# One block for RWKV-7's tables and its scan, whole triangles of T, and one keys product a pair, in a hybrid encoder step

## The reference

```python
def step(S, inp):
    r_t, w_t, k_t, v_t, a_t, b_t = inp
    sa = jnp.einsum('bhij,bhj->bhi', S, a_t)
    S = S * w_t[:, :, None, :] + sa[..., None] * b_t[:, :, None, :] + v_t[..., None] * k_t[:, :, None, :]
    return S, jnp.einsum('bhij,bhj->bhi', S, r_t)
```

## Time and profile before

| what | us |
|---|---|
| median of 3 runs | 3667.14 |
| profiled execution | 3673.35 |
| its span | 3671.6 |
| TensorE, busy | 3480.9 (95%) |
| VectorE, ScalarE, GpSimd, busy | 1516.0, 1133.6, 603.4 |

### The profile page before, as it was taken

One profiled execution on the slowest core, in us unless ns is written; L12 is line 12 of the kernel. 1 busy time (PEld: TensorE's weight loads), 2 busy tenths in 40 slices (PEclk: granted clock), 3 DMA queues, 4 the chain that ended last, 5 costly groups with the idle time before them and its releaser, 6 DMA issues. The chain is left out here.

```text
span 3671.6 us, 60425 instructions
## 1 busy us (share of the span) xinstructions
PE 3480.9 (95%) x25874; PEld 3264.4 (89%) x25874; DVE 1516.0 (41%) x2519; ACT 1133.6 (31%) x2132; POOL 603.4 (16%) x724
## 2 busy tenths in 40 slices
PE   8899979999999999998899996987999999999998
PEld 8898769989999999995598795866998999999997
DVE  6335464343332332335326666555334332232233
ACT  6323263223220220224535532554223321121123
POOL 1100112002110110111312366423101110010012
PEclk9999989999999999998899997999999999999999
DMA  6411311201111111114646777963200111111111
GB/s 224 114 58 60 106 36 49 81 18 41 47 47 47 47 47 46 47 41 117 226 151 204 244 203 162 246 152 83 92 24 29 47 47 47 46 47 47 47 40 66
DMA packets 461158, 323.17 MB, mean 88 GB/s; under 512 B 108871, under 2 KB 438951, under 8 KB 457607
## 3 DMA queue, kind: packets, MB, share of 16 engines
q1 hardware_dynamic: 405645, 280.65, 26.5%
q10 hardware_dynamic: 44878, 19.14, 2.1%
q0 software_dynamic: 10368, 19.51, 1.6%
HBM read 232.32 MB, written 87.01 MB: 87 GB/s over the span
## 5 line engine op out<-in xcount | busy, mean ns | idle before, releaser
L83 PE MATMUL ps<-am_y,am_wh 128*128 128x352 f32 x4944 | 1182.9, 322 | 16.0 <-PEq L2631 16.0
L83 PE MATMUL ps<-am_h,am_wh 128*128 128x352 f32 x3648 | 887.7, 325 | 1.2 <-DVE am_h L1415 1.2
L83 PEld LDWEIGHTS ps<-am_y,am_wh 128*128 128x128 f32 x4944 | 856.4, 188 | 18.1 <-issue 16.8
L83 PE MATMUL ps<-am_y,am_wl 128*128 128x352 f32 x2472 | 792.8, 321 | 0.0
L83 PEld LDWEIGHTS ps<-am_h,am_wh 128*128 128x128 f32 x3648 | 639.8, 189 | 4.3 <-DVE am_h L1415 1.4
L83 PE MATMUL ps<-am_h,am_wl 128*128 128x352 f32 x1824 | 590.4, 324 | 0.0
L83 PEld LDWEIGHTS ps<-am_y,am_wl 128*128 128x128 f32 x2472 | 464.2, 188 | 0.0
L83 PEld LDWEIGHTS ps<-am_h,am_wl 128*128 128x128 f32 x1824 | 344.3, 189 | 0.0
L1503 POOL TENSOR_TENSOR am_silu<-am_silu,rs 128x352 f32<-128x352 f32 x132 | 126.8, 962 | 1229.2 <-ACT am_silu L1359 1229.2
L1085 DVE TENSOR_TENSOR x<-ps,x 128x352 f32<-128x352 f32 x240 | 125.9, 525 | 466.3 <-PE ps L83 460.7
L917 ACT ACTIVATE am_wh<-am_w 128x1024 fp32r<-128x1024 f32 (+1 forms) x184 | 189.5, 1030 | 378.2 <-PE ps L83 372.9
(11 more groups left out here) (340 smaller groups left out, 4581.3 us busy)
## 6 DMA issues: line engine op xcount, KB each, us to landing
am_w<-in_ffn_w SPq DMA_DIRECT2D x120, 512.0 KB, 3.8
rw_ra_d<-tb_rk SPq DMA_DIRECT2D x8, 1056.0 KB, 7.9
rw_kbt_d<-tb_gk SPq DMA_DIRECT2D x8, 1056.0 KB, 4.3
rw_gg_d<-tb_gk SPq DMA_DIRECT2D x8, 1056.0 KB, 6.5
fr_w<-in_xa_wk SPq DMA_DIRECT2D x8, 1024.0 KB, 5.8
fr_w<-in_xa_wv SPq DMA_DIRECT2D x8, 1024.0 KB, 5.4
am_w<-in_xa_wq SPq DMA_DIRECT2D x16, 512.0 KB, 3.8
am_w<-in_xa_wo SPq DMA_DIRECT2D x16, 512.0 KB, 3.8
```

What stands on the lines that cost most here:

```text
L83: mm = nc.tensor.matmul(out, l, part, start=start and n == 0, stop=stop and n == 2)
```

## The change

Tables and scan become one block: `delta_scan` returns its engine programs and some helpers, and `tables` calls them at the end of its own. Scan tiles lie on the other side of SBUF or in tiles of tables; V, A and g/kbt of tables lie in y. T is kept and stored as whole triangles (chunk, s, t), all six stores of the second batch go by ScalarE's queue, and GpSimd waits for them before it loads T. Rows, keys and the first state are loaded ahead, in a new order. `kbt` in the scan gets 128 columns a pair, zero off the two heads' blocks, cleared by GpSimd, filled by DMAs for each head and chunk (256 B pieces); a pair then takes one 128 by 128 product. Behind the scan, bonus and gate have semaphores of their own. One cleanup moves to the end of the layer.

```diff
-def delta_scan(nc, ps, a, ra_d, g_d, kbt_d, vt_d, tt_d, dec, y, p_out, s_out, x, x_d, ln, ident):
+def delta_scan(nc, ctx, spare, stage, ps, a, ra_d, g_d, kbt_d, vt_d, tt_d, dec, y, p_out, s_out, x, x_d, ln, ident):
...
-        g_in, ra_in, kbt, v = (sb(s, SLOTS, PAIRS, 2, HD) for s in ("g_in", "ra_in", "kbt", "v"))
+    sb = lambda s, *shape, side="right": ctx.enter_context(nc.sbuf_tensor(f"ds_{s}", [P, *shape], F32, side=side))
+    state = stage[:, 0:16 * HD].rearrange("r (n p i) -> r n p i", n=2, i=HD)
...
+    g_in, ra_in, v = (sb(s, SLOTS, PAIRS, 2, HD) for s in ("g_in", "ra_in", "v"))
+    kbt = sb("kbt", SLOTS, PAIRS, 2, 2, HD)
+    ra = sb("ra", 2, PAIRS, 2, 2, C)
+    g = spare[:, 0:32 * HD].rearrange("r (s p a h t) -> r s p a h t", s=2, p=PAIRS, a=2, h=2)
+    tt_cleared, v_cleared, keys_cleared = ([sem(f"{t}_cleared{s}") for s in range(SLOTS)] for t in ("tt", "v", "keys"))
...
+    rest_due = lambda l: 16 * (6 * loads(l) - (2 if l % SLOTS == 0 else 0))
...
+    def clear(ops, at):
+        ops.memset(kbt[:, at], 0.0).then_inc(keys_cleared[at], 1)
+        ops.memset(tt[:, at], 0.0).then_inc(tt_cleared[at], 1)
+        ops.memset(v[:, at], 0.0).then_inc(v_cleared[at], 1)
+
+    def first_clears():
+        for l in range(2):
+            clear(nc.gpsimd, l)
+
+    def load_rows(sp, l):
+        c, w = chunks(l)
+        for t, d in ((g_in, g_d), (ra_in, ra_d)):
+            sp.dma_start(t[:, l % SLOTS, :, 0:w, :], d[:, :, c:c + w, :].rearrange("p r c x -> r p c x"))\
+                .then_inc(rows_in[l % SLOTS], 16)
+
+    def load_keys(sp, l):
+        c, w = chunks(l)
+        if l < SLOTS:
+            sp.wait_ge(keys_cleared[l], 1)
+        for h in range(2):
+            r = slice(h * HD, (h + 1) * HD)
+            for sub in range(w):
+                sp.dma_start(kbt[r, l % SLOTS, :, sub, h, :], kbt_d[:, r, c + sub, :].rearrange("p r x -> r p x"))\
                     .then_inc(rest_in[l % SLOTS], 16)
-                if l < SLOTS:
-                    sp.wait_ge(v_cleared[l], 1)
+
+    def load_state(pool):
+        pool.dma_start(of_head[:], a["c_heads"][1]).then_inc(heads_in, 16)
+        pool.dma_start(by_pair(turned[:, 0]), a["state_rwkv"][0, 0].rearrange("h i j -> i h j")).then_inc(init_in, 16)
...
+    def sync(sp):
+        for l in range(LOADS):
+            c, w = chunks(l)
+            if l >= SLOTS:
+                sp.wait_ge(y_done, last(l - SLOTS) + 1)
+            if l >= SLOTS:
+                load_rows(sp, l)
+                sp.wait_ge(y_done, last(l - SLOTS) + 2)
+                load_keys(sp, l)
+            elif l == 1:
+                load_rows(sp, 2)
+                load_keys(sp, 2)
+            if l < SLOTS:
+                sp.wait_ge(v_cleared[l], 1)
+            for h in range(2):
+                sp.dma_start(v[h * HD:h * HD + C, l % SLOTS, :, 0:w, :],
+                             vt_d[:, h * C:(h + 1) * C, c:c + w, :].rearrange("p s c x -> s p c x"))\
...
+    def gpsimd(pool):
+        for l in range(LOADS):
+            if l >= SLOTS:
+                pool.wait_ge(y_done, last(l - SLOTS) + 1)
+            elif l == 2:
+                clear(nc.gpsimd, l)
+            if l < SLOTS:
+                pool.wait_ge(tt_cleared[l], 1)
+            c, w = chunks(l)
+            s, got = l % SLOTS, tt_in[l % SLOTS]
+            for odd in range(2):
                 for h in range(2):
...
-                    for p in range(4 * q, 4 * q + 4):
-                        for h in range(2):
-                            r, at = side[h], p % 4 * HD
-                            mm = nc.tensor.matmul(ps[r, 2 + 2 * q, at:at + HD], kbt[r, l % SLOTS, p, sub, :], vu[r, p, :],
-                                                  start=True, stop=True)
-                    mm.then_inc(s_done, 1)
+                for p in range(4 * q, 4 * q + 4):
+                    at = p % 4 * HD
+                    mm = nc.tensor.matmul(ps[:, 2 + 2 * q, at:at + HD], kbt[:, l % SLOTS, p, sub].rearrange("r h j -> r (h j)"),
+                                          vu[:, p, :], start=True, stop=True)
+                mm.then_inc(s_done, 1)
+            y_part(n, lambda p: vu[:, p, :], lambda p: g[:, s, p, 1], False).then_inc(y_done, 1)
...
@@ tables @@
-        V, A = sb("v", 2, TOK), sb("a", 2, TOK)
+        V, A = y[:, 0:2], y[:, 2:4]
...
-        rk, gk = sb("rk", 2, NCH, HD), sb("gk", 2, NCH, HD)
+        rk = sb("rk", 2, NCH, HD)
+        gk = y[:, 4:8].rearrange("p k t -> p (k t)").rearrange("p (a c x) -> p a c x", a=2, x=HD)
...
-        rows_x = [t.rearrange("l (s x) -> l s x", s=C) for t in eyes]
-        inv_x = [t.rearrange("l s (a t) -> l a s t", a=per[q]) for q, t in enumerate(rows_x)]
+        inv_x = [t.rearrange("l (a s t) -> l a s t", a=per[q], s=C) for q, t in enumerate(eyes)]
...
             sp.wait_ge(bonus_done, p + 1)
             sp.dma_start(pair_rows(bonus_d, p), extra).then_inc(bonus_out, 16)
+            if p == PAIRS - 1:
+                for b in range(BLOCKS):
+                    groups.wait_summed(sp, 3 * KT - 1, b)
+                sp.wait_ge(ra_stored, 16 * PAIRS)
+                sp.wait_ge(g_stored, 16 * PAIRS)
+                sp.wait_ge(kbt_stored, 16 * PAIRS)
+                load_rows(sp, 0)
             sp.wait_ge(vt_out, 4 * (p + 1))
...
-                nc.gpsimd.memset(eyes[q][:, n * C:n * C + (C - 1) * (per[q] * C + 1) + 1:per[q] * C + 1], 1.0).then_inc(eyes_set[q], 1)
+                nc.gpsimd.memset(eyes[q][:, n * C * C:(n + 1) * C * C:C + 1], 1.0).then_inc(eyes_set[q], 1)
...
-                    eng.dma_start(tt_d[p % 2, h, :, p // 2, g0 * per[q]:g1 * per[q]]
-                                  .rearrange("s (g a) t -> g s (a t)", a=per[q]),
-                                  rows_x[q][x_ * rows + g0:x_ * rows + g1]).then_inc(inv_out, 16)
+                    eng.dma_start(tt_d[p % 2, h, p // 2, g0 * per[q]:g1 * per[q]]
+                                  .rearrange("(g a) s t -> g (a s t)", a=per[q]),
+                                  eyes[q][x_ * rows + g0:x_ * rows + g1]).then_inc(inv_out, 16)
...
             store_v(sp, PAIRS - 1)
-            store_triangles(sp, 1, range(3))
+            load_keys(sp, 0)
+            load_rows(sp, 1)
+            load_keys(sp, 1)
+            sp.wait_ge(vt_stored, 64 * PAIRS)
             sp.wait_ge(bonus_out, 16 * PAIRS)
-            sp.wait_ge(inv_out, 16 * 22)
-            sp.wait_ge(vt_stored, 64 * PAIRS)
-            for t in (ra_stored, g_stored, kbt_stored):
-                sp.wait_ge(t, 16 * PAIRS)
             for b in range(BLOCKS):
                 sp.wait_ge(stored[b], beta_due(PAIRS, b))
+            scan_sync(sp)
 
         @block.tensor
         def _(pe):
...
             turn(PAIRS - 1)
+            pe.wait_ge(g_out, len(PIECES) * PAIRS)
+            pe.wait_ge(kbt_out, len(PIECES) * PAIRS)
+            pe.wait_ge(vt_out, 4 * PAIRS)
+            scan_tensor(pe)
...
-            store_triangles(act, 1, range(3, 6))
+            store_triangles(act, 1, range(6))
+            scan_scalar(act)
...
             steps(52, 2 * (C - 1) - top)
+            dve.wait_ge(added[1], steps_done(1, 1, C - 1))
+            dve.wait_ge(ends, PAIRS)
+            for b in range(BLOCKS):
+                groups.wait_summed(dve, 3 * KT - 1, b)
+            scan_vector(dve)
...
                 substitute(pool, nc.gpsimd, 1, n // (C - 1), n % (C - 1))
+            for b in range(BLOCKS):
+                groups.wait_summed(pool, 3 * KT - 1, b)
+            load_state(pool)
+            first_clears()
+            pool.wait_ge(inv_out, 16 * 22)
+            scan_gpsimd(pool)
...
@@ delta_post @@
             for p in range(n):
-                if p >= 2:
-                    sp.wait_ge(gated, 2 * (p - 1))
-                for j, src in enumerate((bonus_d, g_d)):
+                for j, (src, got, free) in enumerate(((bonus_d, bonus_in, shifted), (g_d, gate_in, gated))):
+                    if p >= 2:
+                        sp.wait_ge(free, 2 * (p - 1))
                     for s in range(2):
                         head = p // 2 * 4 + 2 * s + p % 2
                         sp.dma_start(inp[s * HD:(s + 1) * HD, p % 2, j], src[head * HD:(head + 1) * HD, 0:SEQ])\
-                            .then_inc(tile_in[p % 2], 16)
+                            .then_inc(got[p % 2], 16)
                 if p < 2:
...
-                pool.wait_ge(tile_in[p % 2], 64 * (p // 2 + 1))
+                pool.wait_ge(gate_in[p % 2], 32 * (p // 2 + 1))
...
-                dve.wait_ge(tile_in[p % 2], 64 * (p // 2 + 1))
+                dve.wait_ge(bonus_in[p % 2], 32 * (p // 2 + 1))
...
@@ odd_layer @@
-    lt_d, tt_d = (dram("lt0", 2, 5, NCH, C, C), dram("lt1", 2, 3, PADDED, C, C)), dram("tt", 2, 2, C, PAIRS // 2, PADDED, C)
-    with ExitStack() as mix:
+    lt_d, tt_d = (dram("lt0", 2, 5, NCH, C, C), dram("lt1", 2, 3, PADDED, C, C)), dram("tt", 2, 2, PAIRS // 2, PADDED, C, C)
+    with nc.cleanup_on_exit(), ExitStack() as mix:
...
```

(43 more changed lines are left out.)

319 lines of the change are left out of this document (126 added, 193 removed).

## The result

The change makes the kernel **slower**: 3684.13 us (median of 7 runs, 3678.58 to 3689.56) against 3668.15 (7 runs of the kernel before beside it, 3666.09 to 3673.43), a ratio of 1.0041 with a 95% interval of 1.0031 to 1.0050. The forecast was 3655 with a range of 3646 to 3664.

A forecast was written before the change was run, and what follows sets the result against it. Bounds: the tables-to-scan hand-over, a 4.49 us scan-step chain with TensorE stops, then DVE's load waits. -6 + 1.5 - 0.7 + 0 - 7 + 0.4 = -11.8: profiled 3661.5, median about 3655 us; own range 3651 to 3659, with rivals 3646 to 3664.

The forecast's parts named there:

- the fourth, the keys product: Scan step: 8 products of 128 by 128 take 1.11 us, not 1.15; -0.7 us over 33, ends 0 and -1.5.
- Slower: Scan's key loads: a 256 B packet costs twice a 512 B one, DMA queues become the bound; +15, 3682 us; chance 0.08.
- Keys' loads and fetches: Scan: fewer instruction fetches against 256 B key packets, queue share 0.76 to 0.87; 0 us, ends -2 and +4.
- First batch of T: End of tables, ScalarE's queue: ten whole-triangle stores issue at 0.5 us each, 5 us in all; v chain gains 5.
- One block: Hand-over from tables to scan: chunk 1 starts at 2279.5 instead of 2285.4; -6 us, ends -8 and -3.
- the wait of some 6 us for v 1: Scan's start: TensorE ends chunk 0 at 2273.5, then waits for the v load of chunk 1, landed at 2279.5.
- Clock: Scan's first chunks: TensorE's clock may fall again under chunks 1 and 2; +1.5 us, one such stretch about 3.
- Split semaphores: Stage behind the scan: of DVE's 9.9 us of waits for loads, 3 stay; -7 us, ends -4 and -9.
- Cleanup: End of the layer: one cleanup moves there from before the scan; +0.4 us, ends 0 and 0.8.

The follow-up runs named there:

- compact keys: The kernel after with the whole keys part undone (compact key tile, 512 B loads, 16 products of 64 x 64): 3658.9 us, ratio 0.9970 to the kernel before.
- two kernels whose scans have the same records: The kernel after with 64 x 64 keys products, its padded tile and 256 B loads kept (3669.5 us), and after with the whole keys part undone (3658.9 us).

## Why the prediction was wrong

**The step that failed is the fourth, the keys product**: "Products with 128 weight columns are there in the u product, 8 in 1.11 us. 8 at 128 by 128 should take 1.11." It measured 2.00. The row was the right one and was misread: the u products are 64 rows high and alternate between the row halves, so the 1.11 us are the time of four pairs of products side by side, and each by itself takes 223 ns. A whole tile has no other half to run beside. The upper end, "0 (a full-width product costs as much as the pair)", was too low as well, and no rival had this; that the time came near the 3682 of the rival "Slower" is luck, for its queue did not become the bound. The sign of the worth was seen ("the two quadrants already run beside each other") but not that merging them undoes it. The term was -0.7 and is +24 in the steps, +17 by the ratios with only the product put back, and +23.5 for the whole keys part on the kernel before.

**Keys' loads and fetches, 0 taken.** That the queue would not become the bound was right. q1 is 74.5% busy from 2360 to 2420, against 75.9% before and 87% forecast:

```profile
q1 hardware_dynamic: 28590, 10.63, 74.5%
```

It didn't rise because the steps are longer (0.87 x 4.49/5.24 is 0.75); with the same loads and a step of 4.50 it was 93.7%, so 87% was too low. TensorE waited once for v, 2.2 us, which comes on the semaphore that the keys share, but with compact keys it did so too. The fetch stops fell by some 9 us, for a reason the prediction lacked: a slower step hides them. The opened tile costs some 5 to 9 us by the ratios, beyond the end of +4, in the trace mostly by a lower clock, a price that the prediction gave neither the keys' loads nor the opened tile.

**First batch of T, 5 us for ten taken, 13.5 for nine of them measured.**

```profile
2227.09 13.51 ACTq L1971 DMA_DIRECT2D rw_tt_d<-x  x9
2243.15 1.15 ACT L2266 ACTIVATE tb_e<-ps 128x384 f32<-128x384 f32 x3 [16.19 <-DMA rw_vt_d<-tb_e]
```

0.57 us, the first store's time, was carried over to the nine behind it, which took 1.5 each; the other traces show no gain from larger pieces in this batch. V's chain came 1.6 us earlier, not 5.

**One block, -6 taken, -4.8 measured**, largely from another source: the triangles' second batch gives most of it. The order of issues was right: v 1 is issued behind keys 2, and keys 2 behind GpSimd's third clear, 2 us later than worked out:

```profile
2271.63 2.62 SPq L494 DMA_DIRECT2D ds_kbt<-rw_kbt_d  x4
2274.29 2.12 SPq L516 DMA_DIRECT2D ds_v<-rw_vt_d  x4
```

But the wait of some 6 us for v 1 did not come. V 0 was issued at 2265.8 and not by 2261, chunk 0 began at 2271.3 and not 2265.5, took 9.4 us at half clock with its whole keys products, and chunk 1 followed it without a gap. That both ways end near 2280 is luck.

**Clock, +1.5 taken.** Chunk 1 began at half clock (its z rows of 1.07 us are those of chunk 0), but 2300 to 2310 is at 1.00 where the earlier trace rows has 0.69: some 2 us to the good in this trace, not a cost.

**Split semaphores, -7 taken, -4.9 measured** (-5.7 alone), inside its ends. **Cleanup, +0.4 taken**, +1.0 in one trace; what follows the stage took 1153 to 1159 us in all the traces, so this can't be told from nothing.

Without the keys the sum was -11.1 us; the kernel with compact keys measured -0.30% (0.19 to 0.41), which is -11 us. The rest of the forecast held as a sum, its size at the start by luck in good part.

## What to carry to other kernels

Before two products in different parts of the array are merged into one, count the time of a part: here a float32 product with 64 moving columns holds its part for two records, 58 ns each with 64 weight columns and 112 ns with 128, and parts run beside each other. When a row gives n products in t us, ask first how many of them ran at once. And the issue time of the first store of a row is not that of the ones behind it: here it was 0.57 us and then 1.5 each.

## What the runs showed that was not expected

Zero rows in the weights cost TensorE nothing: 128 x 64 tiles that alternate between column halves gave a shorter step (4.35 us) than 64 x 64 ones (4.50). Merely reordering the same sixteen products changed the step by 0.28 us. Ten T stores on ScalarE's queue doubled the issue time of v's four on SyncE's, 3.8 to 8.0 us. The stops beside instruction fetches cost TensorE 3.3 to 9.5 us over 150 us at a step of 4.50 us, and 0.2 us or less at 5.25. And two kernels whose scans have the same records and nearly the same stops were 6.2 us apart there, 4.5 of them by the granted clock.
